# Picking key numbers by rank: one VectorE pass per rank, summed by TensorE in its transposes

## The reference

```python
v1, i1 = lax.top_k(s1, PEER_TOPK)            # 16 best of 128, values and key numbers
v2, i2 = lax.top_k(s2, PEER_TOPK)
cand_score = v1[..., :, None] + v2[..., None, :]            # 256 candidates
cand_idx = i1[..., :, None] * N_KEYS + i2[..., None, :]
top_score, pos = lax.top_k(cand_score, PEER_TOPK)           # 16 of them
experts = jnp.take_along_axis(cand_idx, pos, axis=-1)
gates = jax.nn.softmax(top_score, axis=-1)
```

## Time and profile before

| what | us |
|---|---|
| median of three runs | 3267.96 |
| lowest and highest run | 3267.20, 3270.71 |
| profiled execution, its own time | 3273.78 |
| its span | 3272.0 |
| TensorE busy (matmul) | 3054.9 |
| VectorE busy | 1895.2 |
| ScalarE busy | 1163.4 |
| GpSimd busy | 518.5 |

### The profile page before, as it was taken

How to read it: one execution, slowest core, us unless ns; L and a number is a source line. 1 busy time by engine, 2 the same in 40 slices (tenths; PEclk the granted TensorE clock), 3 DMA queues, 4 the chain that set the end, 5 groups by cost and what they waited for, 6 DMA issues and landing times. The chain is left out here.

```text
span 3272.0 us, 43619 instructions
## 1 busy us (share of the span) xinstructions
PE 3054.9 (93%) x14424; PEld 2467.3 (75%) x14424; DVE 1895.2 (58%) x3607; ACT 1163.4 (36%) x1757; POOL 518.5 (16%) x688
## 2 busy tenths in 40 slices
PE   7999999979897769999999999999996999989998
PEld 5688876868776657888888888888884767866786
DVE  5573444347999968565555555555554674445333
ACT  4443342323337732222222323222223332355222
POOL 1023350004459920000000000000000031024000
PEclk8999999989999989999999999999998989989999
DMA  2210003322223444343334333333332211200322
GB/s 101 77 65 20 27 17 109 110 77 78 84 84 154 191 163 133 116 128 122 122 115 128 115 112 119 128 122 122 118 100 79 90 39 52 97 13 1 117 98 76
DMA packets 137067, 312.52 MB, mean 96 GB/s; under 512 B 9216, under 2 KB 74880, under 8 KB 134784
## 3 DMA queue, kind: packets, MB, share of 16 engines
q1 hardware_dynamic: 136640, 310.74, 28.3%
q10 hardware_dynamic: 320, 0.37, 0.0%
HBM read 273.33 MB, written 37.75 MB: 95 GB/s over the span
## 5 line engine op out<-in xcount | busy, mean ns | idle before, releaser
L180 ACT ACTIVATE split<-raw 128x1024 fp32r<-128x1024 f32 x428 | 442.2, 1053 | 1108.3 <-PE up L1445 458.5
L189 DVE TENSOR_TENSOR split<-raw,split 128x1024 fp32r<-128x1024 f32 x380 | 457.6, 1224 | 476.7 <-ACT split L180 467.1
L1443 PE MATMUL up<-split,weight_high 128*128 128x512 f32 x1024 | 400.7, 391 | 21.2 <-DVE weight_low L2140 21.2
L1444 PE MATMUL up<-split,weight_high 128*128 128x512 f32 x1024 | 399.4, 390 | 0.0
L1445 PE MATMUL up<-split,weight_low 128*128 128x512 f32 x1024 | 399.2, 390 | 0.0
L2286 DVE TENSOR_TENSOR h<-h,up 128x512 f32<-128x512 f32 x416 | 269.4, 684 | 108.1 <-PE up L1445 108.1
L2222 PE MATMUL down<-xh,split 128*128 128x512 f32 x832 | 323.8, 389 | 1.9 <-ACTq L2243 1.9
L2223 PE MATMUL down<-xl,split 128*128 128x512 f32 x832 | 323.7, 389 | 0.0
L2224 PE MATMUL down<-xh,split 128*128 128x512 f32 x832 | 323.6, 389 | 0.0
L2591 POOL TENSOR_TENSOR dec<-dec,upto 128x512 f32<-128x512 f32 x16 | 20.1, 1276 | 1486.0 <-ACT dec L2582 1486.0
L1443 PEld LDWEIGHTS up<-split,weight_high 128*128 128x128 f32 x1024 | 192.8, 188 | 65.1 <-issue 21.4
(11 more groups left out here) (463 smaller groups left out, 5999.6 us busy)
## 6 DMA issues: line engine op xcount, KB each, us to landing
raw<-in_stream SPq DMA_DIRECT2D x440, 512.0 KB, 3.3
gates<-stage SPq DMA_DIRECT2D x16, 2048.0 KB, 6.4
gate<-gates SPq DMA_DIRECT2D x32, 1024.0 KB, 7.2
h<-in_x SPq DMA_DIRECT2D x4, 512.0 KB, 6.0
h<-in_x SPq DMA_DIRECT2D x1, 2048.0 KB, 8.1
rows<-h SPq DMA_DIRECT2D x1, 2048.0 KB, 7.5
h<-rows SPq DMA_DIRECT2D x1, 2048.0 KB, 7.9
out<-res SPq DMA_DIRECT2D x8, 256.0 KB, 2.1
```

The source lines that it names most:

```text
L180: act.activation(g.high[t % slots], g.raw[:, t % RAW, :], ACT.Copy).then_inc(g.high_split, 1)
L189: dve.tensor_tensor(g.low[t % slots], g.raw[:, t % RAW, :], g.high[t % slots], ALU.subtract).then_inc(g.low_split, 1)
L1443: pe.matmul(bank, xh, hi[:, w], start=start, stop=False, skip_group_check=True)
L1444: pe.matmul(bank, xh, lo[:, w], start=False, stop=False, skip_group_check=True)
```

## The change

VectorE no longer builds `hot`. For each rank r from 0 to 15 one instruction compares all 256 ranks of a token with the constant r and multiplies by the key number of that rank, broadcast over the 16 picks. The result is one row `chosen[:, r]` of 256, in which a pick has its key number where its rank is r, and 0 elsewhere. The sum over r is done by TensorE: in the turn, sixteen matmuls per half, with `chosen[:, r]` as weights and the identity as moving operand, add up in the bank. Both are of type fp32r. The gate block, now all that `res` holds, is still transposed. The two halves of the key numbers are now kept one behind the other in `g.keyno`, so that one broadcast covers both; GpSimd's copies in the stage before write to that place. The semaphore counts fall from 16 to 13 per token tile, and a new semaphore counts the sixteen passes.

```diff
-                    for to, src in ((g.vals, best), (g.keyno, where)):
-                        pool.tensor_copy(to[:, :, j, :], src[:, j % 2, :, :]).then_inc(kept, 1)
+                    for to, src, at in ((g.vals, best, j), (g.keyno, where, j % 2 * HEADS + j // 2)):
+                        pool.tensor_copy(to[:, :, at, :], src[:, j % 2, :, :]).then_inc(kept, 1)
...
-    hot = g.at("hot", R, [P, 2, HEADS, TOPK, TOPK])
+    chosen = g.at("chosen", R, [P, TOPK, 2 * hk], F32R)
+    ident_r = g.at("ident_r", R + 16.5, [P, P], F32R)
...
                 def turn(t):
 
-                    pe.wait_ge(step, 16 * t + 16)
+                    pe.wait_ge(chosen_made, TOPK * (t + 1) + 1)
+                    pe.wait_ge(step, 13 * t + 13)
                     if t:
 
                         pe.wait_ge(kept, 3 * t + 1)
-                    for r in range(3):
-                        last = pe.transpose(bank[:, r * P:r * P + P], res[:, r, :], g.ident[:, :])
-                    last.then_inc(turned, 1)
+                    for k in range(2):
+                        for r in range(TOPK):
+                            pe.matmul(bank[:, k * P:k * P + P], chosen[:, r, k * hk:k * hk + hk], ident_r[:, :], start=(r == 0),
+                                      stop=(r == TOPK - 1), skip_group_check=True)
+                    pe.transpose(bank[:, 2 * P:3 * P], res[:, :], g.ident[:, :]).then_inc(turned, 1)
...
                 dve.sem_inc(kept, 1)
+                dve.tensor_copy(ident_r[:, :], g.ident[:, :]).then_inc(chosen_made, 1)
...
-                    dve.wait_ge(step, 16 * t + 10)
-                    for k in range(2):
-                        dve.tensor_tensor(hot[:, k, :, :, :], wide(heads(ranks[:, k, :]), 3),
-                                          g.count[:, 0:TOPK].unsqueeze(1).unsqueeze(1)
-                                          .to_broadcast([P, HEADS, TOPK, TOPK]), ALU.is_equal).then_inc(step, 1)
-                    dve.wait_ge(step, 16 * t + 12)
-                    for k in range(2):
-                        dve.tensor_tensor(hot[:, k, :, :, :], hot[:, k, :, :, :], wide(halves(g.keyno, k), 2),
-                                          ALU.mult).then_inc(hot_made, 1)
-                    for k in range(2):
-                        dve.wait_ge(hot_made, 2 * t + (k + 1))
-                        ins = dve.tensor_reduce(heads(res[:, k, :]), hot[:, k, :, :, :], AX.X, ALU.add)
-                    ins.then_inc(step, 1)
+                    dve.wait_ge(step, 13 * t + 10)
+                    for r in range(TOPK):
+                        dve.scalar_tensor_tensor(
+                            out=chosen[:, r, :].rearrange("p (j k) -> p j k", k=TOPK),
+                            in0=ranks[:, :, :].rearrange("p a (h k) -> p (a h) k", k=TOPK), scalar=float(r),
+                            in1=g.keyno[:, t, :, r].unsqueeze(2).to_broadcast([P, 2 * HEADS, TOPK]),
+                            op0=ALU.is_equal, op1=ALU.mult).then_inc(chosen_made, 1)
                     dve.wait_ge(grown, t + 1)
```

More of the change, by code:

```diff
@@ L1775, in peer_pick @@
     partf = g.at("partf", R + 15, [P, 2, hk])
-    res = g.at("res", R + 15.5, [P, 3, hk])
+    res = g.at("res", R + 15.5, [P, hk])
     total = g.at("total", R + 16.25, [P, 2, HEADS])
     passed = g.sem("passed")
-    ready, counted, picked, step, grown, turned, kept, hot_made = (g.sem(x) for x in (
-        "summed", "counted", "picked", "pick_step", "exp_done", "turned", "kept", "hot_made"))
+    ready, counted, picked, step, grown, turned, kept, chosen_made = (g.sem(x) for x in (
+        "summed", "counted", "picked", "pick_step", "exp_done", "turned", "kept", "chosen_made"))
     per_pick = 5 * HEADS
-    def wide(v, axis):
-        return v.unsqueeze(axis).to_broadcast([P, HEADS, TOPK, TOPK])
     def heads(v):
@@ L1816, in _ @@
                     if j % PER == PER // 2:
-                        act.wait_ge(step, 16 * (j // PER) + 1)
-                        act.activation(res[:, 2, :], res[:, 2, :], ACT.Exp).then_inc(grown, 1)
+                        act.wait_ge(step, 13 * (j // PER) + 1)
+                        act.activation(res[:, :], res[:, :], ACT.Exp).then_inc(grown, 1)
             @block.tensor
@@ L1873, in _ @@
                         keep(t - 1)
-                    dve.tensor_tensor(heads(res[:, 2, :]), best[:, :, :],
+                    dve.tensor_tensor(heads(res[:, :]), best[:, :, :],
                                       best[:, :, 0:1].to_broadcast([P, HEADS, TOPK]), ALU.subtract).then_inc(step, 1)
@@ L1880, in _ @@
                     dve.tensor_scalar(part[:, 1, :], flat, 7, None, ALU.bitwise_and).then_inc(step, 1)
-                    dve.wait_ge(step, 16 * t + 3)
+                    dve.wait_ge(step, 13 * t + 3)
                     dve.tensor_copy(partf[:, :, :], part[:, :, :]).then_inc(step, 1)
-                    dve.wait_ge(step, 16 * t + 4)
+                    dve.wait_ge(step, 13 * t + 4)
                     dve.scalar_tensor_tensor(out=tail_b[:, :], in0=partf[:, 0, :], scalar=9.0, in1=partf[:, 1, :],
@@ L1888, in _ @@
                     dve.tensor_scalar(ranks[:, 0, :], partf[:, 0, :], -1.0, 0.0, ALU.add, ALU.max).then_inc(step, 1)
-                    dve.wait_ge(step, 16 * t + 7)
+                    dve.wait_ge(step, 13 * t + 7)
                     dve.tensor_tensor(ranks[:, 0, :], ranks[:, 0, :], tail_b[:, :], ALU.add).then_inc(step, 1)
                     dve.tensor_tensor(ranks[:, 1, :], partf[:, 1, :], tail_b[:, :], ALU.subtract).then_inc(step, 1)
-                    dve.wait_ge(step, 16 * t + 9)
+                    dve.wait_ge(step, 13 * t + 9)
@@ L1907, in _ @@
+                    for r in range(TOPK):
[4 more added lines that the diff above has]
+                            op0=ALU.is_equal, op1=ALU.mult).then_inc(chosen_made, 1)
                     dve.wait_ge(grown, t + 1)
-                    dve.tensor_reduce(total[:, 0, :], heads(res[:, 2, :]), AX.X, ALU.add).then_inc(step, 1)
@@ L1909, in _ @@
-                    dve.wait_ge(step, 16 * t + 14)
+                    dve.tensor_reduce(total[:, 0, :], heads(res[:, :]), AX.X, ALU.add).then_inc(step, 1)
+                    dve.wait_ge(step, 13 * t + 11)
                     dve.reciprocal(total[:, 1, :], total[:, 0, :]).then_inc(step, 1)
-                    dve.wait_ge(step, 16 * t + 15)
-                    dve.tensor_tensor(heads(res[:, 2, :]), heads(res[:, 2, :]),
+                    dve.wait_ge(step, 13 * t + 12)
+                    dve.tensor_tensor(heads(res[:, :]), heads(res[:, :]),
```

## The result

The changed kernel takes 3279.15 us (median of five runs, 3276.92 to 3285.05). The kernel before, now with five runs, takes 3267.96 (3264.31 to 3270.71). The ratio is 1.0036, with a 95% interval of 1.0022 to 1.0051. The change makes the kernel slower by 11.2 us, 0.36%; the forecast was 3279.3 us. The five runs of the changed kernel spread over 8.1 us, so a forecast that meets the median to 0.2 us owes that closeness to luck.

What follows compares the result with a forecast made beforehand. The prediction took TensorE's instruction list to bound the pick stage: three turns shifting 10.35 us plus 0.9 to 1.0 at VectorE's end make 11.3, so 3267.96 + 11.3 = 3279.3 us; 8-in-10 range 3271 to 3287.

Steps and rivals of the forecast that it cites:

- TensorE bounds the stage, VectorE's saving is worth nothing: Pick stage: its length is TensorE's instruction list; TensorE never waits for VectorE inside it, so VectorE's saving counts 0 us.
- VectorE falls by 44 us: Pick stage: six 2048-element instructions per token tile give way to sixteen 0.42 us passes; 44 us less, 32 to 52.
- A small matmul costs one weight load: In each turn: 32 matmuls of 128 columns at 0.115 us each, the weight load setting the pace; turn 3.79 us.
- Load and columns one after the other, 0.17: Rival for the turn's small matmuls: load and columns in a row, turn 5.55 us, +18.3 us, 3286.3 us; chance 0.08.
- the rival of 0.09: Rival for the turn's small matmuls: loads hide deeper, 0.09 us a step, turn 3.0 us, +8.1, 3276.1 us; chance 0.12.
- The sum: Pick stage: three turns shift the stream by 10.35 us, VectorE's copies end last at 990.3; stage longer by 11.3 us.
- GpSimd is held up for less: Pick stage: beside passes of 0.42 us GpSimd's splits are delayed less; TensorE doesn't wait for them, so 0 us.
- The next stage may open faster: Stage after the pick: TensorE's shorter rest may raise the opening clock, gaining 1.5 us at most; taken as 0.
- The cover of the passes, 1.7 us a rank: Pick stage, between two turns: each of the sixteen passes would have to take over 1.7 us before TensorE noticed.
- VectorE's pace hides in TensorE's record: Rival for the pick's stream: VectorE's big passes slow 512-column matmuls; 7.8 us won back, +3.5, 3271.5 us; chance 0.04.

Runs made afterwards that it cites:

- the lighter VectorE alone: Kernel before, with the changed kernel's sixteen passes but VectorE summing the sixteen rows and TensorE making three transposes: 3266.52 us, ratio 0.9997.
- The half-weight and few-column kernels: Changed kernel, in 30 of 32 small matmuls a turn only 64 weight columns (3273.57 us), or only 64 (3279.24) or 16 (3280.66) moving columns.
- The pauses: Changed kernel with VectorE waiting for its own last pass after every four of sixteen: 3270.6 us, one run; stage 148.8 us against 149.6.
- the estimate above: Passes affordable per rank, from the changed kernel with each pass issued four times: 3327.85 us, ratio 1.0186.

## Why the prediction was right

*TensorE bounds the stage, VectorE's saving is worth nothing.* Right, and shown: the lighter VectorE alone gives 0.9997, and the trace after has the saved time as two waits of VectorE.

*VectorE falls by 44 us.* It fell by 53.9, more than the stated 32 to 52. A pass takes 0.34 us from start to start (5.46 / 16), not 0.42; with GpSimd's splits between them the 64 passes are busy for 24.0 us in the stage, where 26.8 was forecast. The larger part of the miss is that two instructions that used to meet GpSimd's splits mostly no longer do: line 1875 fell from 5.6 to 2.5 us in the stage, line 1912 from 7.0 to 1.2. Neither touches the time.

*A small matmul costs one weight load.* Right: 0.110 us where 0.115 was taken, a turn 3.67 where 3.79 was. The half-weight and few-column kernels show that it is the load. Load and columns one after the other, 0.17, the rival for which the prediction named the rule of the Trainium skill (TensorE: Matmul & The Clock Gate, section The mechanism), is refuted by the same rows. So is the rival of 0.09, and with it the 81 ns of the section Back-to-back issue gap for this type of weights.

*The sum.* Three turns shift the stream by 3 x 3.33 = 10.0 us (10.35 in the forecast). But the last turn began 10.67 us later than before (985.92 against 975.25); the 0.7 us between belong to the next step. The end came from VectorE's copies at 990.46 (990.3). The stage grew by 11.4 us (11.3), the time by 11.2.

*GpSimd is held up for less.* This step failed, and it was priced at 0. The changed kernel's trace beside the earlier trace rows:

```profile
888.54 5.46 DVE L1899 SCALAR_TENSOR_TENSOR chosen<-ranks,keyno 128x256 fp32r<-128x256 f32 x16
...
892.17 4.08 POOL L189 TENSOR_TENSOR split<-raw,split 128x1024 fp32r<-128x1024 f32 x1 [6.78 <-ACT split L180]
```

The argument was that beside passes of 0.42 us GpSimd is held up for less. In sum it is (64.0 us of splits in the stage, 67.2 before). But a split that comes in the middle of the sixteen waits for the last of them: it ends at 896.25, 2.25 us behind the passes, and takes 4.08 us, where the longest before took 3.89. That is just enough to reach TensorE, whose weight loads then wait. The pauses took that away, and 0.7 us with it. The two errors, 0.12 us a turn too much (0.5 us in four turns) and 0.7 us forgotten, went opposite ways, so the forecast hit closer than its steps did. That is luck.

*The next stage may open faster.* It did not. TensorE rested 3.9 us instead of 6.6, and yet the first 5.2 us went at a clock of 0.50, where the earlier trace rows has 0.71:

```profile
993.50:998.70 5.20, 5.09 (x24) 5.12 (x25) 5.20 (x21) 2.73 (x8) 4.79 (x9) 0.50 0.00 0
```

*The cover of the passes, 1.7 us a rank.* Too generous: the estimate above gives 1.4; with passes of 0.34 us it did not matter.

*VectorE's pace hides in TensorE's record.* Refuted: at the full clock, and where no split is late, the stream's matmuls step by 0.227 us whether VectorE is busy for 32.26 of 33 us or for 14.15, and the lighter VectorE alone left the stage at 138.1 us.

## What to carry to other kernels

When two engines are level, look for who waits: here both had a period of 33.0 us, and only one of them would have given time back. Work that is moved to the engine that nobody keeps waiting is paid nearly in full (four turns of 3.33 us are 13.3, and only the 2.5 us by which GpSimd had ended the stage later than VectorE hid a part), so price it by its own rows first; for TensorE that price is the weight load as soon as the moving operand has few columns, and the broad operand belongs on the moving side. A row of short two-input instructions on VectorE can hold GpSimd as long as one big one (a split of 2.4 us took up to 4.7 beside the passes and up to 4.3 beside the big instructions); a pause between them lets it in.

## What the runs showed that was not expected

In a row of matmuls with few moving columns the granted clock can fall without any pause of TensorE: behind a turn with 16 columns in 30 of its 32 matmuls, seven matmuls of 512 columns took 0.43 us each in place of 0.227 and the ones beside them somewhat more than usual, 1.6 us a turn; with 128 columns this never happened.

GpSimd is let in between VectorE's two-input instructions in some cases and not in others. A split that arrives 0.8 us after the first of the sixteen passes starts at once (2.54 us at 855.83 in the changed kernel), and so does one at 1.4 us in the kernel with the lighter VectorE alone (2.59 us); one that arrives 3.6 us after it waits for the last pass. A wait of VectorE for its own semaphore, every four passes, was enough to let it in. What decides between the two cases was not tried.
